# Hybrid attention and mLSTM layer on one core: the small transfers of an attention head on GpSimd's queue, four blocks of x kept in DRAM, softmax steps first in their unit

## The reference

```python
h = rmsnorm(x, norm_w);  proj = h @ w_in          # q,k,v,z of the attention; q,k,v,o,z of the mLSTM; 16 gates
qa = rope_partial(rmsnorm(q_a, q_norm_w))         # 8 heads x 128; the first 32 dimensions are rotated
ka = rope_partial(rmsnorm(k_a, k_norm_w))
# three dilated bands (128,1), (512,4), (2048,16), mixed by their softmax denominators
attn = sum(mix_w[i] * band_attention(qa, ka, va, dil_i)) * silu(z_a)
hm = rmsnorm(mlstm_forward + mlstm_backward)      # 4 heads, qk 128, v 256
hm = sigmoid(o_m) * hm * silu(z_m)
x = x + concat(attn, hm) @ w_out
```

## Time and profile before

| | |
|---|---|
| median of 3 runs | 2060.79 us (2059.7 to 2060.83) |
| the profiled execution | 2060.51 us, of which the span is 2058.4 us |
| PE matmul | 1990.4 us busy, 97% of the span |
| DVE, ACT, POOL | 1300.3 us (63%), 848.7 us (41%), 174.0 us (8%) |
| PE's granted clock, mean | 0.993 of full speed |
| moved by DMA | 281.53 MB, mean 137 GB/s |
| moved in slices 1 to 3 of 40 (of 51 us each) | 160, 182, 179 GB/s |

### The profile page before, as it was taken

The page is one execution under the profiler, slowest core; times in us unless marked ns, Lnnn a source line. Parts: engine busy times, 40 slices in busy tenths (PEclk is TensorE's granted clock), DMA queues, the critical chain, the costliest instruction groups (busy, mean ns, idle before and its releaser), DMA issues.

```text
span 2058.4 us, 27134 instructions
## 1 busy us (share of the span) xinstructions
PE 1990.4 (97%) x9257; PEld 1626.8 (79%) x9257; DVE 1300.3 (63%) x2669; ACT 848.7 (41%) x1350; POOL 174.0 (8%) x156
## 2 busy tenths in 40 slices
PE   4999999999999999999998999999989999999999
PEld 3887788788888888888887878778777787778887
DVE  7777757768768768768778566575665544433222
ACT  5553325335335426335454253644536344242110
POOL 4340000110010010010000111010110000000000
PEclk9999999999999999999999999999999999999999
DMA  4552335564474465375354655364555625425443
GB/s 160 182 179 88 109 113 184 121 151 123 118 166 119 116 161 144 97 180 141 98 199 108 158 138 132 75 154 93 113 121 158 233 66 170 141 74 184 144 153 107
DMA packets 160551, 281.53 MB, mean 137 GB/s; under 512 B 18288, under 2 KB 39312, under 8 KB 160160
## 3 DMA queue, kind: packets, MB, share of 16 engines
q1 hardware_dynamic: 141984, 246.25, 37.3%
q0 software_dynamic: 18432, 33.56, 11.6%
HBM read 185.23 MB, written 92.41 MB: 135 GB/s over the span
## 4 chain that ended last, share of the span: by engine, by line
PE 87%; DVE 4%; issue 3%; ACT 2%; DMA 2%; SPq 1%; DVEq 0%; ACTq 0%
PE ps L714 18%; PE ps L718 18%; PE ps L716 18%; PE ps L742 5%; PE ps L743 5%; PE ps L744 5%; PE ps L925 3%; PE ps L894 2%; PE ps L863 1%; PE ps L819 1%; PE ps L828 1%; PE ps L911 1%; PE ps L822 1%; PE ps L929 1%; DVE w_lo L1190 1%
## 5 line engine op out<-in xcount | busy, mean ns | idle before, releaser
L714 PE MATMUL ps<-t_hi,w_hi 128*128 128x512 f32 x1792 | 717.5, 400 | 48.3 <-DVE t_lo L1644 12.4
L716 PE MATMUL ps<-t_lo,w_hi 128*128 128x512 f32 x1792 | 702.0, 392 | 0.0
L718 PE MATMUL ps<-t_hi,w_lo 128*128 128x512 f32 x1792 | 701.9, 392 | 0.0
L714 PEld LDWEIGHTS ps<-t_hi,w_hi 128*128 128x128 f32 x1792 | 338.8, 189 | 130.5 <-issue 64.1
L718 PEld LDWEIGHTS ps<-t_hi,w_lo 128*128 128x128 f32 x1792 | 338.7, 189 | 72.3
L716 PEld LDWEIGHTS ps<-t_lo,w_hi 128*128 128x128 f32 x1792 | 339.4, 189 | 65.8
L961 ACT CAST w_hi<-w_raw 128x512 fp32r<-128x512 f32 x256 | 158.4, 619 | 417.6 <-PE ps L718 200.8
L961 ACT CAST w_hi<-s_tmp 128x512 fp32r<-128x512 f32 x256 | 158.6, 620 | 268.2 <-PE ps L718 239.6
L1190 DVE TENSOR_TENSOR w_lo<-s_tmp,w_hi 128x512 fp32r<-128x512 f32 x256 | 182.3, 712 | 125.2 <-ACT w_hi L961 115.7
L1190 DVE TENSOR_TENSOR w_lo<-w_raw,w_hi 128x512 fp32r<-128x512 f32 x256 | 181.7, 710 | 119.9 <-ACT w_hi L961 113.5
L742 PE MATMUL ps<-t_hi,w_hi 128*128 128x512 f32 x384 | 155.7, 405 | 9.5 <-DVE xt L1635 9.5
(11 more groups left out here) (215 smaller groups left out, 2667.6 us busy)
## 6 DMA issues: line engine op xcount, KB each, us to landing
w_raw<-w_all_dram SPq DMA_DIRECT2D x320, 256.0 KB, 3.6
fin_dram<-xt SPq DMA_DIRECT2D x128, 256.0 KB, 4.2
fin_dram<-xt POOLq DMA_DIRECT2D x128, 256.0 KB, 4.5
arena<-fin_dram SPq DMA_DIRECT2D x64, 512.0 KB, 6.4
arena<-xT_dram SPq DMA_DIRECT2D x48, 256.0 KB, 5.8
arena<-xT_dram SPq DMA_DIRECT2D x16, 512.0 KB, 4.0
arena<-rs_dram SPq DMA_DIRECT2D x16, 512.0 KB, 5.9
y_raw<-y_dram SPq DMA_DIRECT2D x16, 512.0 KB, 5.1
```

The source lines that it names most:

```text
L714: nc.tensor.matmul(ps[:, bank, :], hi, t_hi[:, n, k, :], start=new and k == 0, stop=False, skip_group_check=True)
L716: nc.tensor.matmul(ps[:, bank, :], hi, t_lo[:, n, k, :], start=False, stop=False, skip_group_check=True)
L718: mm = nc.tensor.matmul(ps[:, bank, :], lo, t_hi[:, n, k, :], start=False, stop=k == KP - 1, skip_group_check=True)
```

## The change

The twelve transfers that prepare a head now stand on POOL's queue (turned_rows): four loads of turned rows, two stores of the roots, two stores of the rotated rows to a new rot_dram, and per tensor one spread load of roots and one load of rotated rows back. For this the 32 rotated dimensions are interleaved (TURNED, in the weights, the norm weights and the cos and sin tables), so that the partner is two partitions away. normed moves to 8 and 9. v gets a place of its own (v_at), loaded at 4 and scaled at 7; z is scaled at 10. The softmax pieces of DVE and ACT stand at the head of the unit, before evict. The blocks n = 1, 3, 4, 5 of build 0 are stored to t_dram in units 16 to 44, high and low, and loaded in units 332 to 336 in place of being built a second time. Some semaphores are merged (B12, B22 and B21 have one for four tiles; counters of the gates).

```diff
@@ -90,6 +90,10 @@
...
+KEPT = (1, 3, 4, 5)
...
@@ -195,6 +199,7 @@
...
+        v_at = view(5504, 1024)
...
@@ -388,7 +392,7 @@
...
-                             ).then_inc(b21_in if blk == B21 else b_in[blk][kt], 16)
+                             ).then_inc(b11_in[kt] if blk == B11 else b_in[blk], 16)
...
@@ -428,18 +432,37 @@
...
+            def flat_t(t, n):
+                return t[:, n].rearrange("p k s -> p (k s)").bitcast(F32)
...
+            def t_stores(u):
+                i, rest = divmod(u - 16, 8)
+                if rest in (0, 4) and 0 <= i < len(KEPT):
+                    n = KEPT[i]
+                    sp.wait_ge(tl_done[n], t_made(n, 0))
+                    sp.dma_start(t_dram[i, rest // 4], flat_t((t_hi, t_lo)[rest // 4], n)).then_inc(t_out, 16)
...
+            def t_loads(u):
+                off = u - BUILD_AT[2]
+                if off - 2 in KEPT:
+                    n = off - 2
+                    i = KEPT.index(n)
+                    sp.wait_ge(prod, PRODUCTS * (STAGE[2] - 1) + n + 1)
+                    for part_, t in enumerate((t_hi, t_lo)):
+                        sp.dma_start(flat_t(t, n), t_dram[i, part_]).then_inc(t_in[i], 16)
...
             def build_loads(b, off):
...
@@ -505,59 +527,31 @@
...
-                        sp.wait_ge(tl_done[1], t_made(1, 2))
-                        sp.wait_ge(tl_done[5], t_made(5, 2))
-                        sp.wait_ge(tl_done[3], t_made(3, 2))
-                        sp.wait_ge(tl_done[4], t_made(4, 2))
+                        sp.wait_ge(tl_done[0], t_made(0, 2))
+                        sp.wait_ge(tl_done[2], t_made(2, 2))
...
+                        sp.wait_ge(m_out, 16 * M_HEADS)
...
-                        sp.dma_start(eps_rows[0:2 * TB], eps_dram).then_inc(eps_out, 16)
+                        sp.dma_start(eps_rows[0:2 * TB], eps_dram).then_inc(rows_out, 16)
...
-                        sp.wait_ge(a_vtr, 3 * h)
...
-                if at == 2:
+                if at == 4:
...
-                        sp.wait_ge(a_t, 16 * h)
-                    for i, to in enumerate(turn):
-                        src = fin[2 * GROUPS[g[i]][0] + 1 - i]
-                        for k in range(4):
-                            sp.dma_start(to[k * ROT:(k + 1) * ROT, 0:256],
-                                         src[k // 2, 0:ROT, k % 2 * 256:(k % 2 + 1) * 256]).then_inc(turn_in[i], 16)
-                if at == 3:
-                    sp.wait_ge(a_rs, h + 1)
-                    for i in range(2):
-                        sp.dma_start(rs_dram[h, i].rearrange("r b n -> b r n"),
-                                     qk_rs[i * TB:(i + 1) * TB].rearrange("p (r n) -> p r n", r=CLASSES)
-                                     ).then_inc(rs_out, 16)
-                if at == 5:
-                    sp.wait_ge(rs_out, 32 * (h + 1))
-                    sp.wait_ge(a_ss, h + 1)
-                    for i, to in enumerate((a_q, a_k)):
-                        sp.dma_start(to, rs_dram[h, i].rearrange("r b n -> (r b n)").unsqueeze(0).to_broadcast([P, SEQ])
-                                     ).then_inc(bc_in, 16)
-                if at in (5, 6):
-                    i = at - 5
-                    raw, to = ((raw_a, turn[0]), (raw_b, turn[1]))[i]
-                    sp.wait_ge(a_rot, 8 * h + 4 * i + 4)
-                    for k in range(4):
-                        sp.dma_start(raw[0:ROT, k * 256:(k + 1) * 256], to[k * ROT:(k + 1) * ROT, 0:256]
-                                     ).then_inc(turned[i], 16)
+                        sp.wait_ge(a_pv, 4 * h)
+                    tile_done(sp, g[0], 0)
+                    sp.dma_start(halves(v_at), fin_tile(g[0], 0)).then_inc(v_raw, 16)
...
-                if at == 8:
-                    sp.wait_ge(a_rope, 2 * h + 1)
-                    tile_done(sp, g[0], 0)
-                    sp.dma_start(halves(raw_a), fin_tile(g[0], 0)).then_inc(v_raw, 16)
...
@@ -633,6 +627,8 @@
...
+                    t_stores(u)
+                    t_loads(u)
...
@@ -703,7 +699,9 @@
...
-                if g in STAGE and not (g == 0 and n < 2):
+                if g == STAGE[2] and n in KEPT:
+                    pe.wait_ge(t_in[KEPT.index(n)], 32)
+                elif g in STAGE and not (g == 0 and n < 2):
...
@@ -1000,14 +997,17 @@
...
+                if b == 1 and n in KEPT:
+                    act.wait_ge(t_out, 32 * len(KEPT))
...
-                    if off == at:
+                    if off == at and (b, blk) != (2, B12):
...
-                if off in (1, 3, 4, 5, 6, 8, 9):
-                    t_high(b, {1: 0, 3: 2, 4: 1, 5: 3, 6: 4, 8: 6, 9: 5}[off])
+                n = {1: 0, 3: 2, 4: 1, 5: 3, 6: 4, 8: 6, 9: 5}.get(off)
+                if n is not None and not (b == 2 and n in KEPT):
+                    t_high(b, n)
...
@@ -1125,6 +1125,8 @@
                 if at == 13:
                     act.wait_ge(a_zs, h + 1)
                     nc.scalar.activation(ystage, ystage, ACT.Silu).then_inc(a_z, 1)
+
+            def softmax_act(h, at):
                 if 0 <= at - 12 < 8:
                     normalised(h, at - 12)
                 if 0 <= at - 13 < 8:
@@ -1144,12 +1146,14 @@
...
             for u in range(UNITS):
+                for h in range(ATT_HEADS):
+                    softmax_act(h, u - A_START[h])
...
                     evict(u - 1)
...
@@ -1278,24 +1280,31 @@
...
+                if b == 1 and n in KEPT:
+                    dve.wait_ge(t_out, 32 * len(KEPT))
...
+                if b == 1:
+                    build_sums(off)
+                n = {1: 0, 3: 2, 4: 1, 5: 3, 6: 4, 8: 6, 9: 5}.get(off)
+                if n is not None and not (b == 2 and n in KEPT):
+                    t_low(b, n)
+
+            def build_sums(off):
...
@@ -1542,8 +1551,8 @@
...
-                dve.wait_ge(turned[i], 64 * (h + 1))
-                dve.wait_ge(bc_in, 32 * (h + 1))
+                dve.wait_ge(turned[i], 16 * (h + 1))
+                dve.wait_ge(bc_in[i], 16 * (h + 1))
...
@@ -1569,25 +1578,36 @@
...
-            def attention_dve(h, at):
+            def take_probs(g, i):
+                dve.wait_ge(a_t, 16 * g + 2 * i + 2)
+                if i % 2 == 0 and i > 0:
+                    dve.wait_ge(a_pv, 4 * g + i // 2)
+                nc.vector.tensor_copy(pT[:, 4:6, (i % 2) * P:(i % 2 + 1) * P],
+                                      ps[:, 3, 0:256].rearrange("p (b q) -> p b q", q=P)).then_inc(a_td, 1)
...
+            def softmax_dve(h, at):
...
+                if 0 <= at - 13 < 8:
+                    take_probs(h, at - 13)
...
+            def attention_dve(h, at):
...
-                if at == 8:
+                if at == 10:
...
-                if at == 10:
+                if at == 7:
...
-                    nc.vector.tensor_tensor(raw_a, raw_a, xrs[:], ALU.mult).then_inc(a_vs, 1)
+                    nc.vector.tensor_tensor(v_at, v_at, xrs[:], ALU.mult).then_inc(a_vs, 1)
...
-                        dve.wait_ge(eps_out, 32)
+                        dve.wait_ge(rows_out, 96)
...
@@ -1602,8 +1622,8 @@
...
-                if at in (7, 9):
-                    normed(h, (at - 7) // 2)
+                if at in (8, 9):
+                    normed(h, at - 8)
...
@@ -1652,6 +1665,8 @@
...
             for u in range(UNITS):
+                for h in range(ATT_HEADS):
+                    softmax_dve(h, u - A_START[h])
...
                     evict(u - 1)
...
@@ -1729,10 +1744,47 @@
...
+            def turned_rows(h, at):
+                g = A_FINAL[h]
+                if at == 2:
+                    if h > 0:
+                        pool.wait_ge(a_t, 16 * h)
+                    tile_done(pool, g[0], 1)
+                    tile_done(pool, g[1], 0)
+                    for i, to in enumerate(turn):
+                        src = fin[2 * GROUPS[g[i]][0] + 1 - i]
+                        for k in range(2):
+                            pool.dma_start(to[k * 2 * ROT:(k + 1) * 2 * ROT, 0:256],
+                                         src[k, 0:ROT].rearrange("r (q n) -> (r q) n", q=2)).then_inc(turn_in[i], 16)
+                if at == 3:
+                    pool.wait_ge(a_rs, h + 1)
+                    for i in range(2):
+                        pool.dma_start(rs_dram[h, i].rearrange("r b n -> b r n"),
+                                     qk_rs[i * TB:(i + 1) * TB].rearrange("p (r n) -> p r n", r=CLASSES)
+                                     ).then_inc(rs_out, 16)
+                if at in (5, 6):
+                    i = at - 5
+                    pool.wait_ge(rs_out, 32 * (h + 1))
+                    pool.wait_ge(a_ss, h + 1)
+                    pool.dma_start((a_q, a_k)[i], rs_dram[h, i].rearrange("r b n -> (r b n)").unsqueeze(0)
+                                 .to_broadcast([P, SEQ])).then_inc(bc_in[i], 16)
+                if at in (4, 5):
+                    i = at - 4
+                    pool.wait_ge(a_rot, 8 * h + 4 * i + 4)
```

(12 more changed lines are left out.)

116 lines of the change are left out of this document (53 added, 63 removed).

## The result

| | before | after |
|---|---|---|
| median of the runs compared | 2059.70 us (5 runs) | 2044.96 us (5 runs, 2042.88 to 2049.95) |
| profiled execution, span | 2060.51, 2058.4 us | 2042.88, 2041.1 us |

The ratio is 0.9934, its 95% interval 0.9917 to 0.9952: 0.66% faster, 13.6 us of 2060; the two medians are 14.7 us apart. The forecast was 2034 us, 27 us faster, with a range of 2022 to 2053. Sign and range hold; about half of the gain came.

The account below looks back on a forecast made before the run. PE, busy 97% of the span, was taken to lose time only in waits, mainly behind DVE's waits for DMA. Terms 24.9 + 3 + 5 = 33 us won, 6 charged, 27 us: 2034 us, range 2022 to 2053.

Parts of the forecast that it names:

- What bounds the kernel: PE is busy 97% of the span; only its waits can be won, mainly evictions behind DVE's waits for DMA.
- The waits for the copies: Attention heads: rows by DRAM on POOL's queue and later uses win 24.9 us, less 6.4 charged for slow landings.
- rival 2: Rotated rows: two trips are too slow, 8.3 us lost a head at 8.0 us a landing; 2095 us, chance 0.09.
- Rival 1: DMA: the 16 engines are the limit, not the queue; only the later product helps; 2045 to 2056 us, chance 0.14.
- Softmax order: Attention units: softmax pieces before eviction and weight split win 3 us of 4.1 us of PE's waits.
- Kept blocks: Last build: four blocks reloaded instead of made again remove PE's waits there, 5 us won; reload charged nothing.
- rival 3: Last build: the reload collides at 276 GB/s, PE waits 6 us at n = 5; 2041 us, chance 0.11.
- What would show it: Signs: marks about 82 us apart in all heads, no DVE wait over 1 us for rot_dram, no PE wait on t loads.

Follow-up runs that it names:

- out_first: Changed kernel with DVE's output addition ahead of its unit's attention work in the output stage: 2037.7 us, ratio 0.9897 to the kernel before.
- soft_late: Changed kernel with the softmax pieces of DVE and ACT back behind eviction and weight split: 2049.7 us, ratio 0.9954 to the kernel before.
- before_later: Kernel before with only the first product moved from unit 7 to 8 and z's use from 8 to 10: 2043.0 us, ratio 0.9922.
- onehop: Changed kernel with transfers on SP and rotated rows straight SBUF to SBUF in eight copies: 2029.8 us, ratio 0.9859 to the kernel before.
- on_sp: Changed kernel with its twelve small transfers per head issued by SP, at the same units: 2035.2 us, ratio 0.9883 to the kernel before.

## Why the prediction was right, and where it was wrong

*What bounds the kernel.* Right: PE's waits on evictions and additions that stand behind a wait of DVE for a DMA; out_first, which moves nothing but that order, won 7.6 us. Wrong in part: I read this on head 4 and took heads 5 and 7 to be the same. There the last wait ahead of the addition was that for z, 2.43 and 2.67 us. The earlier trace rows had these waits, and I gave only head 0's to z.

*The waits for the copies, 24.9 less 6.4.* By the ratios 7 to 8 us came of these 18.5: 13.6 in all, less the 4 of the softmax order and the 2 of the kept blocks. The marks say where. Head 0 gave 1.5, head 4 7.2 (soft_late takes 2.4 of it back, so that much is the softmax order's) and head 6 4.7, against 2.1, 8.4 and 5.9 forecast; heads 5 and 7, forecast at 8.5, together gave -0.7. The later uses are worth just these 8.5 there when the transfers stay as they were (before_later). The step that failed is the price of the new way of the rows, two landings of 4.3 us with 0.8 charged per head. In heads 5 to 7 the stores of the rows took 4.7 to 7.0 us and the first return 6.2 to 7.3, so that the product of heads 5 and 7 began 13.4 and 13.5 us after the rotation where it had begun 9.5 and 9.2 before. The 4.3 was taken from POOL's added stores, which lie spread over the kernel, and not from the stretch in which these transfers run. The text had both broadcasts "ahead of the returns on the same queue" in rival 2 and gave them no price in the sum; the return in head 5 was issued 1.1 us late behind one of them and the second store. POOL's standing for the rs stores (3.4 to 4.6 us a head there) had no price either; it ended about when the rows' own store landed, or before, and cost the first return little.

*Where the gain came from.* I gave the move to POOL and the later uses one sum. The runs part them: the later uses of the product and z alone are 16 us (before_later), and the changed kernel with the rows straight on SP is 29 us faster than before (onehop); the transfers as changed take 15 of these back (0.0075 of 2060).

*Rival 1, the engines are the limit,* came nearest in number, with 2045 at its lower end, at a chance of 0.14, and that is luck in part. It said that the queue makes no difference, and on_sp shows 10.5 us of difference. That the rows land late when the engines are full is borne out. Against it I had put that part of the delay was SP's order; the runs point the other way: the rows came sooner by SP's queue than by POOL's in both pairs of runs, and waits on SP that hold back its bulk loads help them. The Trainium skill's sentence (DMA: Bandwidth & Descriptors, Issuing engines are not separate DMA queues) agrees with the runs as far as it goes, since no run gained by the second issuer. That it cost 8.4 and 10.5 us here is the measurement's to say.

*Rival 2.* Its break-even, two landings of 5.9 us each, was reached in heads 5 to 7 (12.0, 11.7 and 11.9 us for store and first return). Heads 5 and 7 lost by it what the later use of z would have won; but heads 0 to 4 together took 9.5 us less than before, where it had 4.1 lost in each. Its rule on the shared port (the Trainium skill, SBUF — State Buffer, SBUF: two separate sides) finds no support: POOL's issues of the returns took 0.561 us in the median and 0.867 at most.

*Softmax order, 3 us.* Measured 4 (soft_late), with intervals that overlap. Right in size as far as that shows, though head 2 still has a wait of 2.2 us, on line 1556: the second product, not the order, is late there, and in onehop it is gone.

*Kept blocks, 5 us.* The profile says 3.4, the ratios 2. One wait of 1.19 us for t_dram stands at n = 5, and up to 2.9 in other runs: rival 3 in small, at which the sum had nothing.

*What would show it.* "No wait of DVE over 1 us for arena<-rot_dram" failed (29.1 us in 8 waits, 8.2 the longest), marks of 82 us held in heads 1 and 3 alone.
